# Gate weights as 16 columns, gate rows spread by transposes, and a reordered start and attention loop in a two-layer decoder kernel

## What is computed

```python
z = jnp.einsum('bsd,dp->bsp', h, w_in)
mq, mk, mv, mo, mi, mf, aq, ak, av, ga, gb = split_columns(z)
qk = jax.nn.silu(causal_depthwise_conv(jnp.concatenate([mq, mk], axis=-1), conv_w, conv_b))
...
y_a = h_a @ w_branch_a            # mLSTM over chunks of 128 tokens, gates mi (input) and mf (forget)
...
l_own = jnp.einsum('bhqd,bhkd->bhqk', qq, own_k).astype(f32) * scale \
    + bias_hb[:, t5_bucket(qpos[:, None] - own_pos[None, :])]
...
y = jax.nn.sigmoid(ga) * y_a + jax.nn.sigmoid(gb) * y_b
return y @ w_out
```

## Time and profile before

| what | us |
|---|---|
| median of 3 runs | 1624.34 |
| profiled execution | 1623.83 |
| its span, first to last instruction | 1622.0 |
| TensorE busy | 1582.1 |
| VectorE busy | 1278.6 |
| ScalarE busy | 1100.4 |
| issue of one small load on GpSimd | 0.54 |
| small loads from GpSimd in the start, issue to landing | 5.4 to 5.9 |
| one function table load on ScalarE | 1.28 |

### The profile page before, as it was taken

One profiled execution on the slowest core, in us unless ns is written; L12 is line 12 of the kernel. 1 busy time (PEld: TensorE's weight loads), 2 busy tenths in 40 slices (PEclk: granted clock), 3 DMA queues, 4 the chain that ended last, 5 costly groups with the idle time before them and its releaser, 6 DMA issues.

```text
span 1622.0 us, 23424 instructions
## 1 busy us (share of the span) xinstructions
PE 1582.1 (98%) x7577; PEld 1305.8 (81%) x7577; DVE 1278.6 (79%) x1549; ACT 1100.4 (68%) x1359; POOL 33.3 (2%) x43
## 2 busy tenths in 40 slices
PE   6999999999999898999999999999999999999998
PEld 5886878888788686788888888888888888888887
DVE  4865564554576656888989989999999999989997
ACT  5546654444555665677877877777777877878875
POOL 1000010000000000000000000000000000000000
PEclk9999999999999999999999999999999999999999
DMA  8544455555345447699999999999999999999991
GB/s 302 177 137 153 141 198 190 185 196 169 122 156 177 152 152 278 223 385 372 367 394 364 379 391 358 384 390 351 398 382 351 400 384 343 406 381 346 406 412 74
DMA packets 208114, 467.51 MB, mean 288 GB/s; under 512 B 14169, under 2 KB 16353, under 8 KB 208017
## 3 DMA queue, kind: packets, MB, share of 16 engines
q1 hardware_dynamic: 202880, 452.57, 75.5%
q0 software_dynamic: 4080, 13.79, 2.3%
q10 hardware_dynamic: 1056, 0.03, 0.0%
HBM read 458.46 MB, written 7.88 MB: 288 GB/s over the span
## 4 chain that ended last, share of the span: by engine, by line
PE 91%; DVE 4%; ACT 3%; issue 1%; DMA 0%; SPq 0%; DVEq 0%; ACTq 0%
PE pA L510 76%; PE pB L510 8%; PE pB L529 3%; DVE w_lo L1298 1%; ACT w_hi L988 1%; PE pA L563 1%; PE pA L529 0%; DMA aqk<-mlstm_norm_g_dram 0%; PE pA L882 0%; PE pB L684 0%; ACT L1137 0%; ACT L1128 0%; DVE small L1444 0%; ACT aqk L1137 0%; ACT ga L1128 0%
## 5 line engine op out<-in xcount | busy, mean ns | idle before, releaser
L1298 DVE TENSOR_TENSOR w_lo<-raw,w_hi 128x1024 fp32r<-128x1024 f32 x570 | 668.6, 1220 | 133.0 <-ACT w_hi L988 126.3
L988 ACT ACTIVATE w_hi<-raw 128x1024 fp32r<-128x1024 f32 x570 | 577.2, 1058 | 115.6 <-PE pA L510 77.2
L510 PE MATMUL pA<-w_hi,hT_hi 128*128 128x512 f32 (+1 forms) x1376 | 542.9, 395 | 1.8 <-DVE hT_lo L1319 1.2
L510 PE MATMUL pA<-w_hi,hT_lo 128*128 128x512 f32 (+1 forms) x1376 | 533.4, 388 | 0.0
L510 PE MATMUL pA<-w_lo,hT_hi 128*128 128x512 f32 (+1 forms) x1376 | 532.5, 387 | 0.0
L510 PEld LDWEIGHTS pA<-w_hi,hT_lo 128*128 128x128 f32 x1376 | 258.3, 188 | 54.1
L510 PEld LDWEIGHTS pA<-w_hi,hT_hi 128*128 128x128 f32 x1376 | 258.7, 188 | 52.2 <-DVE hT_lo L1319 1.4
L510 PEld LDWEIGHTS pA<-w_lo,hT_hi 128*128 128x128 f32 x1376 | 258.9, 188 | 49.8 <-issue 0.2
L1298 DVE TENSOR_TENSOR w_lo<-more,w_hi 128x1024 fp32r<-128x1024 f32 x224 | 262.3, 1219 | 11.6 <-ACT w_hi L988 11.6
L988 ACT ACTIVATE w_hi<-more 128x1024 fp32r<-128x1024 f32 x224 | 230.5, 1059 | 21.8 <-PE pA L510 20.7
L510 PE MATMUL pA<-w_hi,ex_hi 128*128 128x512 f32 x440 | 172.7, 393 | 0.0
(11 more groups left out here) (310 smaller groups left out, 1367.0 us busy)
## 6 DMA issues: line engine op xcount, KB each, us to landing
raw<-expert_w_gate_dram SPq DMA_DIRECT2D x160, 512.0 KB, 5.9
raw<-expert_w_up_dram SPq DMA_DIRECT2D x128, 512.0 KB, 6.0
raw<-expert_w_down_dram SPq DMA_DIRECT2D x96, 512.0 KB, 6.1
raw<-w_in_dram SPq DMA_DIRECT2D x44, 1024.0 KB, 5.0
more<-expert_w_down_dram SPq DMA_DIRECT2D x88, 512.0 KB, 5.4
more<-expert_w_up_dram SPq DMA_DIRECT2D x80, 512.0 KB, 6.4
more<-expert_w_gate_dram SPq DMA_DIRECT2D x56, 512.0 KB, 6.5
toep<-expert_w_down_dram SPq DMA_DIRECT2D x40, 512.0 KB, 5.8
```

Of the source, the lines that this page charges most:

```text
L510: ins = mm(o, r if swap else l, l if swap else r, start=first and n == 0, stop=True, skip_group_check=True)
L988: f(w_hi[:, m % PARTS, :], raw_slot(m), ACT.Copy).then_inc(s["w_hi_done"], 1)
L1298: tt(w_lo[:, m % PARTS, :], raw_slot(m), w_hi[:, m % PARTS, :].bitcast(F32), ALU.subtract).then_inc(s["w_lo_done"], 1)
```

## The change

Gate weights' hi and lo halves lie side by side in one tile of 16 columns, so two matmuls a block do what three did; the two halves of the result are added afterwards. The gate rows are spread by transposes of one column read with step zero. The start is reordered: SyncE asks for the first weights right behind x and the identity, in two halves and a whole load; other constants come later; GpSimd loads the gate weights after a wait for the second half, and all its bias loads stand behind it; TensorE gets 13 and 5 matmuls of zeros; pieces 0 and 1 stand ahead of the gate columns. The bias table is built in the other direction and read with step -1, and its flip is gone. Logits are made for two heads at a time. Gates 7 and 8 stand elsewhere on ScalarE.

```diff
-        wg_hi = sb("wg_hi", [P, KT, 8], F32R)
-        wg_lo = sb("wg_lo", [P, KT, 8], F32R)
+        wg = sb("wg", [P, KT, 16], F32R)
+        wg_hi, wg_lo = wg[:, :, 0:8], wg[:, :, 8:16]
...
-            sp.wait_ge(s["in_vec"], 16 * 9)
-            sp.wait_ge(s["in_wg0"], 16)
...
+            def first_chunk():
+
+                wv = w_in[0].rearrange("(k p) n -> p k n", p=P)
+                for q, landed in enumerate((s["first_landed"], w_loaded[0])):
+                    sp.dma_start(raw_slot(q).rearrange("p (k n) -> p k n", k=2),
+                                 wv[:, 2 * q:2 * q + 2, Q0:Q0 + COLS]).then_inc(landed, 16)
+                load(1, wv[:, 4:8, Q0:Q0 + COLS], 4)
...
+            g.wait_ge(w_loaded[0], 16)
+            g.dma_start(wg_raw[:], wif[0]).then_inc(s["in_wg0"], 16)
...
-            skew = bass.AP(bias_rows.tensor, 0, [[1, P], [BT, AH], [1, S]])
+            skew = bass.AP(bias_rows.tensor, BT - P - S + 1, [[1, P], [BT, AH], [1, S]])
...
+                    mm(B2[0:16, 0:S], wg[:, k, :], hT_hi[:, k, :], start=(k == 0), stop=True, skip_group_check=True)
+                    ins = mm(B2[0:8, 0:S], wg_hi[:, k, :], hT_lo[:, k, :], start=False, stop=True,
+                             skip_group_check=True)
...
-                chunks(0, 1)
+                at = 1 if layer else 3
+                if layer == 0:
+                    chunks(0, 2)
+                    pe.wait_ge(s["vec_ready"], 1)
+                    narrow(2 * layer, layer + 1)
+                    chunks(2, 3)
+                else:
+                    chunks(0, 1)
                 narrow_turns(layer + 1).then_inc(s["gate_psum"], 1)
-                chunks(1, 4)
+                chunks(at, 5 - layer)
...
                 for a in range(A):
-                    ins = mm(pB[:, 2 + a, :], block_of(ONES), Wt[:, a].rearrange("p h s -> p (h s)"),
-                             start=True, stop=True)
+                    for h in range(MH):
+                        c = MH * a + h
+                        ins = turn(pB[:, 2 + a, P * h:P * (h + 1)], RR[:, c:c + 1].broadcast_to([P, P]), h == 0)
...
-                for h in range(AH):
+                for pair in range(AH // 2):
+                    h = 2 * pair
                     turn_probs(h)
                     chunks(34 + h, 35 + h)
-                    if h + 2 < AH:
-                        logits(h + 2)
+                    turn_probs(h + 1)
+                    if pair + 1 < AH // 2:
+                        logits(pair + 1)
                     weigh(h)
+                    chunks(35 + h, 36 + h)
+                    weigh(h + 1)
...
+                gate(7)
                 split_to(m0 + 32 + AHEAD)
...
+                    if h == 3:
+                        gate(8)
...
-                    eng.wait_ge(s["lg_psum"], n + 1)
+                    eng.wait_ge(s["lg_psum"], n + 2 - h % 2)
...
+                    rel = toep[:, h, ::-1]
+                    stt(l[:, 0:P], o[:, 0:P], float(AD) ** -0.5, rel[:, P:S], ALU.mult, ALU.add)
+                    link(stt(l[:, P:P + S], o[:, P:P + S], float(AD) ** -0.5, rel, ALU.mult, ALU.add))
```

More of the change, by code:

```diff
@@ L381, in _ @@
                 for i, c0 in enumerate(CHUNK_COLS):
+                    if layer == 0 and i == 0:
+                        first_chunk()
+                        other_constants()
+                        continue
                     k_major(w_in[layer], (M0[layer] + 4 * i) // 2, c0, COLS)
@@ L422, in _ @@
             g.dma_start(ids[:], token_ids).then_inc(s["in_ids"], 16)
+            g.wait_ge(s["vec_zero"], 1)
+            for r, src in ((R_QG, q_norm_g), (R_KG, k_norm_g)):
+                for half in range(2):
+                    g.dma_start(vec_rows[r:r + NL, AD * half:AD * (half + 1)], src).then_inc(s["in_qk"], 16)
             g.wait_ge(s["brow_ready"], 1)
@@ L529, in turn, with keep_warm @@
                 return mm(o, src, ident, is_transpose=True, start=first, stop=True, skip_group_check=True)
-            pe.wait_ge(s["in_cst"], 16)
-            pe.wait_ge(s["in_vec"], 16 * 9)
-            turn(B4[:, 0:P], vec_rows).then_inc(s["vec_psum"], 1)
+            pe.wait_ge(s["parts_zero"], 1)
+            def keep_warm(n):
+                for i in range(n):
+                    mm(B0, g_lo[:, 0, 0:P], g_lo[:, 0, 0:512], start=True, stop=True)
+            keep_warm(13)
+            pe.wait_ge(s["in_ident"], 16)
+            pe.wait_ge(s["in_gain"], 16)
+            mm(B3[:, R_MIXG:R_FFNG], vec_rows[R_MIXG:R_FFNG, :], ident[R_MIXG:R_FFNG, R_MIXG:R_FFNG],
+               is_transpose=True, start=True, stop=True, skip_group_check=True).then_inc(s["vec_psum"], 1)
             def keep_going(n):
@@ L1055, in mixer @@
                     after(m0 + 4 * i + 3)
+                    if layer == 0 and i == 1:
+                        eng.wait_ge(s["vec_psum"], 2)
+                        f(vec[:, R_FFNG:NVEC], B4[:, R_FFNG:NVEC], ACT.Copy).then_inc(s["vec_ready"], 1)
                     f(conv_in[:, 4 * i:4 * i + 4, TAPS - 1:],
@@ L1103, in mixer, with gate @@
                 split_to(m0 + 29 + AHEAD)
+                def gate(i):
+                    after(m0 + 4 * i + 3)
+                    i2 = i - 7
+                    dst = ga if i2 < 2 else gb
+                    f(dst[:, :, 512 * (i2 % 2):512 * (i2 % 2 + 1)], pA[:, 2 * (i % 2):2 * (i % 2) + 2, :],
+                      ACT.Sigmoid).then_inc(s["lin_evac"], 1)
                 for b in range(2):
@@ L1343, in mixer @@
                 pre = PRE.rearrange("p (a g) -> p a g", a=A)
-                link(tt(pre, bank_as(B3, A, 8), gbias[:, layer:layer + 1, :].broadcast_to([P, A, 8]), ALU.add))
+                both = bank_as(B3, A, 16)
+                link(tt(pre, both[:, :, 0:8], gbias[:, layer:layer + 1, :].broadcast_to([P, A, 8]), ALU.add))
+                link(tt(pre, both[:, :, 8:16], pre, ALU.add))
                 ip, fp = pre[:, :, 0:MH], pre[:, :, MH:]
@@ L1358, in mixer @@
                 link(nc.vector.tensor_copy(BC, B5[:, 0:8]))
-                link(tt(rr, ip, bc, ALU.subtract))
-                for a in range(A):
-                    for h in range(MH):
-                        ins = ts(Wt[:, a, h, :], ident, RR[:, MH * a + h:MH * a + h + 1], None, ALU.mult)
-                ins.then_inc(s["diag_ready"], 1)
+                tt(rr, ip, bc, ALU.subtract).then_inc(s["rr_ready"], 1)
                 split_to(m0 + 6 + AHEAD)
@@ L1385, in mixer @@
                 eng.wait_ge(s["lin_evac"], NCH * layer + 2)
+                if layer == 0:
+                    eng.wait_ge(s["vec_ready"], 2)
                 for t in range(2 * MH):
@@ L1589, in top @@
                 link(stt(hot, iota_b, -8.0, wide(idx), ALU.add, ALU.is_equal))
-            link(nc.vector.tensor_copy(lg, bank_as(B3, A, 8)))
+            both = bank_as(B3, A, 16)
+            link(nc.vector.tensor_copy(lg, both[:, :, 0:8]))
+            link(tt(lg, both[:, :, 8:16], lg, ALU.add))
             top(m1, hot1)
@@ L1778, in tables @@
     hot = ((np.arange(buckets)[:, None] == bucket) & past).astype(np.float32)
-    mask = np.broadcast_to(np.where(past, 0, NEG).astype(np.float32), (AH, BT)).copy()
+    mask = np.broadcast_to(np.where(past, 0, NEG).astype(np.float32), (AH, BT))
+    hot, mask = [np.ascontiguousarray(t[:, ::-1]) for t in (hot, mask)]
     return c.reshape(P, 8 * P), hot, mask, ids
```

133 lines of the change are left out of this document (61 added, 72 removed).

## The result

The changed kernel takes **1597.26 us** (median of 4 runs, 1597.17 to 1600.52) against 1623.82 us (4 runs, 1622.35 to 1624.86): a ratio of 0.9842, 95% interval 0.9825 to 0.9859. The forecast was 1599.0 us, with a range of 1594 to 1606. The profiled execution took 1597.17 us, with a span of 1595.3 at a mean granted clock of 0.999; before it was 1623.83 and 1622.0.

What follows compares the result with a forecast made beforehand. TensorE, busy 98% of 1622.0 us, was taken as the bound, with most to win in layer 0's head. Savings 9.3 + 5.4 + 9.8 + 0.8 = 25.3; 1623.83 - 25.3 = 1598.5, plus 0.5: 1599.0 us; range 1594 to 1606.

Steps and rivals of the forecast that it cites:

- First weight piece near 11, piece 8 near 43: Head of layer 0: first weight piece near 11 us, piece 8 done at 42.6 instead of 51.98, saving 9.3 us.
- rival (a): Head of layer 0: gate weights land late, gate columns start at 21.3, 3.5 us more, 1602.5; chance 0.13.
- The flip, 5.4: Bias table in layer 0: removing four full-precision matmuls, a 1.88 us copy and their waits saves 5.4 us.
- stretch at half clock beside the flip: Layer 0 beside the bias table's flip: the 5.4 us saved there includes a stretch at half clock.
- Reversed read of the table: 0, ends 0 and 2: VectorE additions reading the bias table backwards: taken to cost 0 us, ends 0 and 2.
- Loop: 2.5 + 0.6 + 1.8 = 4.9 a layer: Attention loop: paired logits save 2.5, fewer mode changes 0.6, two waits on exponentials 1.8; 9.8 us for both layers.
- Rival (b): Attention loop turns from TensorE to its helpers: waits stay, about 0.8 more each pair; 2 x 3.5 lost, 1606; chance 0.10.
- Small gate work, 0.8: Layer 1 and router: 0.23 from fewer gate matmuls plus 0.57 from the ones-matmuls, 0.8 us; router nets nothing.
- I forecast no such fall in the waiting path: Head of layer 0: no fall of granted clock to 0.50, as the old head had from 21 to 24 us.
- rival (c): Head of layer 0: first two pieces at half clock, 1.8 us each, partly hidden under the gate load; 1601; chance 0.05.
- rival (e): Weight pieces of layer 0: idle stretches after warming matmuls bring lasting half clock, 1.8 us a piece; 1635; chance 0.04.
- Expert stage as a block: Expert stage: its weight loads are released by earlier work, so it moves forward unchanged in length and gives nothing back.

## Why the prediction held, step by step

- **First weight piece near 11, piece 8 near 43.** Held: 11.18 and 41.60. The gate columns' start was forecast at 17.8 from the nearest landing, 8.3 us. The load was asked for at 9.58, 1.3 us later than assumed, but took 6.5 us, not 8.3, and the columns followed piece 1 at once, at 17.19. The eight transposes took 0.87, not 1.15, and the gate columns 1.87. The head gave 10.4 instead of 9.3, just above its range's end of 10.3.
- **The gate load as the price of the head**, rival (a). It did not decide here, but the mechanism is real: a load asked for 3.3 us later brought 3.3 us on TensorE, as (a) had it.
- **The flip, 5.4.** Measured 4.9. The step "Layer 1 has the same program ... and is my measure" is nearly right: layer 0 has a wait of its own, 0.43 us ahead of piece 18 (24.72 us for 108 matmuls in the chain above, then a new link at 66.46), for low parts; VectorE is busy without a break from 47.4 us to there. In layer 1 the same 120 matmuls run through. The "stretch at half clock beside the flip" was part of the gain, up to 1.7 us of it, as the text said; with the flip back it returned, longer.
- **Reversed read of the table: 0, ends 0 and 2.** Held. The two additions of a head on VectorE take 0.28 and 0.42 us now, against 0.29 and 0.42 in the kernel before (medians of 16).
- **Loop: 2.5 + 0.6 + 1.8 = 4.9 a layer.** Measured 5.1. Single logits alone gave 2.9 back, for the 3.1 of matmul time; what is left, 2.2, is the waits (2.3 to 0.5) and small steps. The terms are right as a sum in this order of undoing only. The prediction priced the gates' move as a gain of 1.8. The runs show that it is what makes the pairs pay: without it pairs lose 3.9 and 5.2 us in the two layers against the old loop, up to 3.4 and 5.1 of it half clock (medians 1619.62 and 1609.92). Rival (b) had this mechanism and its sign, at "one more of about 0.8 at each pair", without the clock; its price of 3.5 a layer is not the sum of its own terms.
- **Small gate work, 0.8.** Measured 1.1: 0.85 from the spread (0.57 had been taken, since the eight transposes were priced at 1.15), 0.2 from the gate columns, as experiment (0.2) and forecast (0.23) have it.
- **Half clock.** "I forecast no such fall in the waiting path" held in the profiled execution: the steps are those of the full clock from 11 us on. But the ground given for it did not. "In the old head the granted clock was 1.00 up to 21 us" took the column at its word: the old head's first transposes took 3.42 us, where the same 16 take 2.11 behind the warming matmuls. The experiment without warming matmuls has slow steps under a shown 1.00, so rival (c), "Half clock in the first two pieces", is what would have come without the warming matmuls. The rule of the Trainium skill, "TensorE: Matmul & The Clock Gate" (Part 1, What's actually happening), that throttled is the default, is borne out at the start. It also says that activity releases the clock, and the 13 warming matmuls, slow themselves (5.00 us), are followed by full-rate pieces in the changed kernel. The forecast had no term for them, and without them piece 8 ends 2.7 us later: that this line of the sum held is the kernel's doing and, for the forecast, luck. Piece 0 at 4.64 us in the earlier trace rows is the same clock at its lower level a second time: the old gate columns had run at 0.12 a step, and after a wait of 1.64 us the steps went to 0.21 at 21 us.
- **Slower, rival (e).** Nothing for it in the changed kernel. The experiment with the gates back is the nearest thing: 20.5 us at half clock, a price of up to 10.2. The "1610 + 25" of its price does not follow from its terms; 20 pieces at 1.8 on top of 1599 give the same 1635.
- **Expert stage as a block.** Held, 0.1 us.

The miss in the span is 1.1 (head) - 0.5 (flip) + 0.2 + 0.2 (loops) + 0.3 (gate work) + 0.1 (rest) = 1.4 us. The forecast of 1599.0 is 1.7 above the median: this 1.4, and most of the 0.5 that was added for the distance of median and profiled execution. In the changed kernel that distance is 0.1, and a fourth run of the kernel before, 1622.35, has brought its median to 1623.82.

## What to carry to other kernels

Price a reordering and the move that goes with it together: ask what stood between a result and its use in the old order, and what else stands in the producer's queue there. A wait of 2 to 3 us on TensorE was followed in most variants here by 3.4 or 6.8 us at half clock, which cost up to 1.7 or 3.4 us on top, so a small load or a table load on its path deserves more care than its duration says. When a first stretch looks fast by the granted clock, check it by the step between like matmuls.

## What the runs showed of the hardware

- The granted clock shown as 1.00 at a program's start is not evidence of the upper level. Steps between equal matmuls were 0.21 us there and 0.12 later, both under 1.00.
- Half-clock stretches come and go behind one and the same wait. The wait of 2.6 us ahead of the query transposes has one of 3.4 us behind it in eight of the variants, in one of the two layers each; the changed kernel, its repeat and the kernel with single logits have none. With the gates back, of the waits on exponentials those of 2.65, 2.65 and 2.46 us have a stretch behind them and one of 2.45 has none. Two of nine runs of the changed kernel were about 3 us longer, at a mean clock of 0.998 against 0.999. What decides it stays open.
- Transposing a column read with step zero costs what a dense one costs (0.11 us, eight in 0.87), and VectorE's read of 256 elements backwards what a forward one does (0.42 us in both).
